# Down projection in seven block products for its first 1024 columns, with three changes of waits

## The chip, the cores and the metric

The kernel runs on the 8 cores of one Trainium2 chip. Each core computes one of 8 batch elements with the same program and exchanges nothing with the others. The metric is the device time of the slowest core in microseconds (us), as the median of several executions. The engines are named as in the profile: PE is TensorE, DVE VectorE, ACT ScalarE, POOL GpSimd, SP the queue of SyncE. POOL and SP issue the DMAs here.

## What is computed

One layer: token mixing (one projection of 2048 tokens to 9216 columns, a gated unit and block-sparse attention, an output projection), cross-attention to 256 memory tokens, and a SwiGLU block, each with RMSNorm before and after. The part that is changed most is the last matrix product.

```python
def swiglu(n, w_gate, w_up, w_down):
    return (jax.nn.silu(n @ w_gate) * (n @ w_up)) @ w_down
# n (2048 tokens, 2048), w_gate and w_up (2048, 5632), w_down (5632, 2048)
h = h + rms_norm(swiglu(rms_norm(h, ffn_pre_g), w_gate, w_up, w_down), ffn_post_g)
```

## The kernel before

The work runs in stages, in the trace in this order: input projection (to about 1003 us), attention with the memory's K and V and w_a as filler (to 1283), branch b (to 1394), output projection (to 1640), cross-attention (to about 1850), gate and up projections (to 2874), down projection (to the end). Operands are f16, sums f32 in PSUM, a bank holding 128 x 512. Every instruction goes through helpers of the Builder class (`mm` L315, `tr` L318, `act` L328, `tt` L331, `cp` L348 and L350, `dma` L357), so rows are told apart by their tiles.

**Order.** `Sched.add` keeps a program order for each engine and works out waits from Buf objects. Each engine runs its list in order, so an instruction that waits holds back all behind it. A write to a Buf that another DMA with another semaphore wrote last waits for that DMA. The stages from attention to cross-attention are ordered by `Plan.run`, a list scheduler: each task has an engine, a duration, a latency (`lat`, for a DMA the guessed time to landing), dependencies and a priority. The plan sets only the order on each engine; real waits are by semaphore. Input, gate/up and down projections are written out by hand.

**Seven products.** Input, gate and up projections already use a Strassen form (Winograd's variant). A block pair is 2 x 2 on each side; operands are A11, A12, A22, A21, the sums S1, S2, S3 (in A21's place), S4, and for the weights B11, B21, B22, T1, T2, T3 (in B12's place), T4. `quad_steps` (L947) runs the seven products of 8 matmuls of 512 columns into three banks X, Z, Y; after the first, third and fifth product into X and the fourth into Y, ACT copies the bank out (`snap`), the product goes on accumulating, and DVE adds bank and copies into the four results. It is a generator that yields after its first and second product. `mid` holds hooks that are called after the n-th product, for sums that DVE makes beside it. Results are stored when done.

**Attention's start** (`last_block`, L1210). While the last block of the input projection runs, SP issues K, Q and V of head 0 and then the four 1 MB tiles wk (weights for the memory's K and V). `f_hl` (L1354) loads K, Q and V of head 1, with lat 8. `wkl` (L1554) stands for the four wk loads in the plan; `wal` loads w_a, both first tiles at once.

**Cross-attention's start.** `f_wo` (L1932) loads the two column halves of w_co into one tile `wo` with one Buf; all output products depend on both (`lo`). `gto`, the gains that DVE needs in every eviction, is loaded after them in plan order.

**Gate and up.** 22 blocks of 256 columns, each loaded by POOL for gate and up; p is the half of the tokens (p=1 the later 1024). The loop over `quads` (L2272) begins with four quads with p=1 alone, since the plan before has done two blocks with p=0; ahead of it DVE makes the sums S1 to S4 of p=1 (`fsum`, two instructions each). Beside it POOL casts w_down to f16 in DRAM (`wd_cast`, 128 rows each time, 44 times, into WDH). The hidden values go to DRAM as HIDT, one row of 11,264 bytes per partition and token tile.

**Down.** All 2048 columns are plain: out(128 tokens, 512 columns) is 44 matmuls of 512 columns. The loop over `units` (L2323) has two parts. The first is 32 column blocks (columns 0 to 1023 of 16 token tiles), in 28 units, most with one column block, each with its own load of an `ht` tile (1408 KB) into one of three buffers; ACT copies each bank out, and it is stored to Y3. Weights lie in three sets of 44 tiles of 128x512 (W0, W1, W2), loaded in parts by POOL from WDH in runs of 1 KB. The second part goes over 16 token tiles with the column blocks 2 and 3; Y3 and the residual H2 come back (`row_pre`), and the norm and the sum are finished there.

## Time and profile before

| what | value |
|---|---|
| times of the three runs | 3480.22, 3475.23, 3486.62 us |
| median | 3480.22 us |
| the profiled execution's own time | 3503.88 us |
| its span, on core 5, the slowest | 3502.3 us |
| spans of all cores | 3456.9 to 3502.3 us |
| PE busy | 3406.8 us, 97% of the span |
| DVE, ACT, POOL busy | 1474.6, 1214.1, 237.4 us |
| matmuls of the down projection | 2816, mean 380 ns on the page |
| DMA packets' bytes | 467.89 MB |

A span is the time from the first to the last instruction of one core. Matmuls are pipelined: the duration of one (380 ns) is longer than the distance to the next (216 ns), so the cost of many is read from where a long piece starts and ends. "Idle before, releaser" is time in which the engine waited, and what ended that.

### The profile page before, as it was taken

How to read it: one execution, taken by the hardware profiler on the slowest of the kernel's cores; microseconds unless marked ns; L12 is line 12 of the kernel's file. 1: busy time of each engine (PE TensorE's matmuls, PEld its weight loads, DVE VectorE, ACT ScalarE, POOL GpSimd, SP SyncE). 2: the span in 40 equal slices, each digit the busy share in tenths (PEclk: the TensorE clock that was granted, in tenths of full speed). 3: DMA queues.
4: the chain of work that ended last, by engine and by line, in shares of the span. 5: the costliest groups of instructions: out<-in, count | busy, mean ns of one | idle time of the engine just before them, and what ended most of it. 6: DMA issues, size and time to landing. Idle time of an engine off the chain costs nothing.

```text
span 3502.3 us, 50752 instructions; the slowest of 8 cores (3456.9 to 3502.3 us)
## 1 busy us (share of the span) xinstructions
PE 3406.8 (97%) x17866; PEld 1646.4 (47%) x17866; DVE 1474.6 (42%) x2704; ACT 1214.1 (35%) x2179; POOL 237.4 (7%) x318
## 2 busy tenths in 40 slices
PE   6999999999989999999999999999999999999998
PEld 3544444444456654545744444444444444444443
DVE  4754246533237767444875343434433420001222
ACT  4643322344357740444862223232232220000111
POOL 1100000000000000000111000000000000000000
PEclk9999889999999999999999999999999999999999
DMA  7446666767663544544779767787677858577775
GB/s 177 104 67 84 94 95 109 122 111 139 107 164 90 122 135 126 164 143 163 217 199 108 86 84 94 93 93 93 76 95 90 97 156 270 151 218 210 212 223 164
DMA packets 341576, 467.89 MB, mean 134 GB/s; under 512 B 29904, under 2 KB 289232, under 8 KB 319184
## 3 DMA queue, kind: packets, MB, share of 16 engines
q0 software_dynamic: 192240, 157.30, 35.7%
q1 hardware_dynamic: 149088, 307.35, 29.7%
q8 instruction: 148, 2.42, 0.3%
q14 instruction: 100, 0.82, 0.1%
HBM read 486.62 MB, written 154.14 MB: 183 GB/s over the span
## 4 chain that ended last, share of the span: by engine, by line
PE 90%; DMA 5%; DVE 2%; issue 1%; ACT 1%; POOL 0%; SPq 0%; DVEq 0%; ACTq 0%; POOLq 0%
PE ps L315 89%; PE ps L318 1%; DMA xs<-x 1%; DMA wv<-w_in 1%; DMA H<-yr 1%; DMA ht<-HIDT 1%; DMA k<-KD 1%; DMA VD<-stg 0%; DMA gto<-gains 0%; DVE f L331 0%; DVE n1op L331 0%; ACT stg L348 0%; DVE at L341 0%; ACT no L328 0%; ACT nbh L328 0%
## 5 line engine op out<-in xcount | busy, mean ns | idle before, releaser
L315 PE MATMUL ps<-wd,ht 128*128 128x512 f16 x2816 | 611.1, 380 | 4.2 <-DMA ht<-HIDT 4.2
L315 PEld LDWEIGHTS ps<-wd,ht 128*128 128x128 f16 x2816 | 276.0, 98 | 339.1 <-issue 8.9
L348 ACT COPY fpf<-ps 128x512 f32<-128x512 f32 x336 | 197.0, 587 | 558.8 <-PE ps L315 558.8
L348 ACT COPY pf<-ps 128x512 f32<-128x512 f32 x256 | 150.3, 587 | 285.1 <-PE ps L315 285.1
L331 DVE TENSOR_TENSOR fpf<-ps,fpf 128x512 f32<-128x512 f32 x168 | 115.9, 690 | 315.5 <-PE ps L315 315.5
L315 PE MATMUL ps<-n1op,ws0r 128*128 128x512 f16 x1024 | 241.5, 390 | 2.5 <-DVE n1op L331 1.7
L315 PE MATMUL ps<-n1op,ws1r 128*128 128x512 f16 x1024 | 240.3, 389 | 0.0
L315 PE MATMUL ps<-RBH,ma 128*128 128x512 f16 x1024 | 226.2, 379 | 0.0
L328 ACT ACTIVATE pT<-ps 128x512 bf16<-128x512 f32 (+1 forms) x320 | 169.3, 543 | 73.8 <-PE ps L315 70.1
L315 PE MATMUL ps<-n1op,ws0t 128*128 128x512 f16 x768 | 183.0, 390 | 2.8 <-DVE n1op L331 1.8
L315 PE MATMUL ps<-n1op,ws1t 128*128 128x512 f16 x768 | 181.1, 387 | 0.9 <-ACT pf L348 0.6
L331 DVE TENSOR_TENSOR fpf<-fpf,fpf 128x512 f32<-128x512 f32 x84 | 58.2, 692 | 269.0 <-ACT fpf L348 269.0
L315 PE MATMUL ps<-f,fw1r 128*128 128x512 f16 x736 | 168.0, 379 | 2.2 <-DVE sm L2008 2.2
L315 PE MATMUL ps<-f,fw0r 128*128 128x512 f16 x736 | 168.1, 379 | 1.5 <-ACT fpf L348 1.5
L328 ACT ACTIVATE junk<-ps 128x512 bf16<-128x512 f32 x128 | 76.4, 597 | 264.8 <-PE ps L315 261.2
L315 PEld LDWEIGHTS ps<-n1op,ws0r 128*128 128x128 f16 x1024 | 101.6, 100 | 129.8 <-issue 33.5
L315 PEld LDWEIGHTS ps<-n1op,ws1r 128*128 128x128 f16 x1024 | 102.0, 100 | 125.8 <-issue 23.7
L331 DVE TENSOR_TENSOR yrow<-yrow,gtf 128x1024 f32<-128x1024 f32 x16 | 19.5, 1219 | 322.3 <-ACT dj L328 322.3
L315 PE MATMUL ps<-f,fw2r 128*128 128x512 f16 x672 | 151.9, 379 | 0.9 <-ACT fpf L348 0.9
L315 PEld LDWEIGHTS ps<-RBH,ma 128*128 128x128 f16 x1024 | 99.0, 98 | 113.6
L315 PE MATMUL ps<-f,fw3r 128*128 128x512 f16 x672 | 151.9, 379 | 0.0
L315 PE MATMUL ps<-at,was 128*128 128x512 f16 x512 | 150.4, 379 | 0.0
(224 smaller groups left out, 4634.3 us busy)
## 6 DMA issues: line engine op xcount, KB each, us to landing
ht<-HIDT SPq DMA_DIRECT2D x44, 1408.0 KB, 10.7
H<-yr SPq DMA_DIRECT2D x32, 1024.0 KB, 10.7
HIDT<-ffo SPq DMA_DIRECT2D x88, 256.0 KB, 5.7
WDH<-w_fd POOLq DMA_DIRECT2D x44, 512.0 KB, 20.9
ws0r<-w_in POOLq DMA_DIRECT2D x16, 1024.0 KB, 14.7
ws1r<-w_in POOLq DMA_DIRECT2D x16, 1024.0 KB, 14.5
GS<-stgh SPq DMA_DIRECT2D x64, 256.0 KB, 6.5
xr<-x SPq DMA_DIRECT2D x16, 1024.0 KB, 8.6
```

Source lines behind the costliest of these rows:

```text
L315: self.S.add("pe", lambda e: e.matmul(out, lhsT, rhs, start=start, stop=stop, **kw), reads, writes)
L318: self.S.add("pe", lambda e: e.transpose(out, in_, ident), reads, writes)
L328: self.S.add("act", lambda e: e.activation(out, in_, func, **kw), reads, writes)
L331: self.S.add(eng, lambda e: e.tensor_tensor(out, in0, in1, op), reads, writes)
L348: self.S.add("act", lambda e: e.copy(out, in_), reads, writes)
```

## The change

WDH shrinks to columns 1024 to 2047. Columns 0 to 1023 of w_down go to WD7, laid out by half of the rows (kh) and 256 columns, so that one of its blocks is 11,264 contiguous bytes per partition; each cast of 128 rows becomes two DMAs. The first part of the down stage becomes 16 calls of `down_quad`. One takes two token tiles (rows 1 and 2 of A) and 512 columns: its operands are quarters, 128 x 2816 elements (22 tiles of 128 of the hidden dimension). Each product is 22 matmuls of 256 columns. A quad loads four quarters of 704 KB, two quads ahead, and DVE makes the next quad's four sums. The weights' seven operands are three sums (`wt`) and four loaded blocks (`w7`); the first set is loaded and summed during the last gate/up quads, the second loaded in quads 1 to 4 and summed in quad 7. Columns 1024 to 2047 are computed as before, with weights W2 (loaded in quads 9 to 12) and W3 (in quad 15), three ht buffers, and an extra load order there.

The three changes of waits. Attention: two of the four wk loads come after head 1's K, Q and V, whose lat is 15; the first w_a load reads the Buf of the last wk tile. Cross-attention: the two halves of `wo` have their own Bufs, and each product depends on its half. Gate/up: before the first quad only S1 and S2 are made, quads 0 and 1 run their first two products each in turn, then S3 and S4 are made, and then the rest of both.

The core of the diff:

```diff
-    WDH = B.scratch("WDH", [HID, D], F16)
+    WDH = B.scratch("WDH", [HID, 1024], F16)
+    WD7 = B.scratch("WD7", [2, 4, 128, HC // 2 * 256], F16)
...
-        for i in range(4):
-            B.dma("sp", wk.t[i][:], WKH[i], wk.d[i], bWKH, [wk.b[i]])
+        for i in range(2):
+            load_wk(i)
+    def load_wk(i):
+        B.dma("sp", wk.t[i][:], WKH[i], wk.d[i], bWKH, [wk.b[i]])
...
-        hld.append(T("sp", 1.5, f_hl, [hld[-1]], hstart[h - 1], [(QK, ("qk", h))], lat=8.0))
+        hld.append(T("sp", 1.5, f_hl, [hld[-1]], hstart[h - 1], [(QK, ("qk", h))], lat=15.0 if h == 1 else 8.0))
...
-    wkl = [T("sp", 0.0, lambda: None, (), 0, lat=6.0 + 3.0 * i) for i in range(4)]
+    wkl = [T("sp", 0.0, lambda: None, (), 0, lat=1.0 + 4.0 * i) for i in range(2)]
+    wkl += [T("sp", 0.5, lambda i=i: load_wk(i), (), 0.1 * i, lat=6.0 + 4.5 * i) for i in (2, 3)]
...
-            cast_load(was.t[i][:].rearrange("p (k n) -> p k n", k=8), w_a, 0, GW, jp * 256, 256, was.d[i], [was.b[i]])
+            B.dma("pool", was.t[i][:].rearrange("p (k n) -> p k n", k=8),
+                  w_a[:, jp * 256:(jp + 1) * 256].rearrange("(k p) n -> p k n", p=128), was.d[i], [wk.b[3]] if jp == 0 else [],
+                  [was.b[i]])
...
-        wal.append(T("pool", 1.2, wa_load(jp), wal[-1:], FILL + jp, [(WAP, ("wa", jp))], lat=10.0))
+        wal.append(T("pool", 1.2, wa_load(jp), wal[-1:] or wkl[3:], FILL + jp, [(WAP, ("wa", jp))], lat=10.0))
...
+        return lambda: B.dma("sp", WO3[:, ch],
+                             WOH[:, ch * 1024:(ch + 1) * 1024].rearrange("(k p) n -> p k n", p=128), dwo[ch], bWOH, [wo_t.bufs[ch]])
+    lo = [T("sp", 0.5, f_wo(ch), [own], -7 + ch, lat=6.0 + 2.5 * ch) for ch in range(2)]
...
+                        B.mm(p[:], ap[:, hh * 128:(hh + 1) * 128], WO3[:, cb // 2, hh, cb % 2 * 512:(cb % 2 + 1) * 512], hh == 0, hh == 3,
+                             bufs + [wo_t.bufs[cb // 2]], [pb])
+                o_ = T("pe", 0.87, f_o, [oc, o_ if cb else None, lo[cb // 2]], tt, [(BY, bk)] + ([(YR, yk), (SM, sk2)] if cb == 0 else []),
...
+        kh, kk = r // KD2, r % KD2
+        B.dma("pool", WD7[kh, :, :, kk * 256:(kk + 1) * 256].rearrange("c p n -> p c n"),
+              w_fd[r * 128:(r + 1) * 128, 0:1024].rearrange("p (c n) -> p c n", c=4), dw7[r % 4], [], [bWD7[r]])
+        B.dma("pool", WDH[r * 128:(r + 1) * 128, :], w_fd[r * 128:(r + 1) * 128, 1024:2048], dwd[r % 4], [], [bWDH[r]])
...
+    W2 = WCol("wd2", [(0, 11), (122880, 11), (134144, 11), (145408, 11)])
+    W3 = WCol("wd3", [(163840, 11), (18432, 11), (156672, 5), (11264, 5), (120832, 1), (52224, 11)])
+    hts = [tile("ht%d" % i, o_h, HC * 128, F16, claim=False) for i, o_h in enumerate((98304, 29696, 40960))]
...
+    def hop(m, w):
+        if w in (S1, S2, S4):
+            return hs[(S1, S2, S4).index(w)]
+        return rq[m % 2][(A11, A12, A21, A22).index(w)]
+    def load_q(m, w, claim=False):
+        t_ = hop(m, w)
+        if claim:
+            t_.claim()
+        tt, kh = 2 * (m % 8) + (w in (A21, A22)), int(w in (A12, A22))
+        B.dma("sp", t_[:], HIDT[tt, :, kh * HH:(kh + 1) * HH], t_.d,
+              [bHID[b][tt // 4] for b in range(kh * NBF // 2, (kh + 1) * NBF // 2)], [t_.b])
+    def load_w7(g, i, after=()):
+        kh, c = i // 2, 2 * g + i % 2
+        B.dma("pool", w7[g][i][:], WD7[kh, c], w7[g][i].d, bWD7[kh * KD2:(kh + 1) * KD2] + list(after), [w7[g][i].b])
+    def hsum(m, which):
+        o, a_, b_, op = ysum[which]
+        O, A_, B_ = hop(m, o), hop(m, a_), hop(m, b_)
+        B.tt(O[:], A_[:], B_[:], op, [A_.b, B_.b], [O.b])
+    def wsum(g, which):
+        b11, b12, b21, b22 = w7[g]
+        O, A_, B_ = {"T1": (wt[0], b12, b11), "T3": (b12, b22, b12), "T2": (wt[1], b22, wt[0]), "T4": (wt[2], b21, wt[1])}[which]
+        for c in range(2):
+            cs_ = slice(c * WH // 2, (c + 1) * WH // 2)
+            B.tt(O[:, cs_], A_[:, cs_], B_[:, cs_], ALU.subtract, [A_.b, B_.b], [O.b])
     def pre_down():
-        W0.claim()
-        W0.load(0)
-        hts[0].claim()
-        load_unit(0)
+        for t_ in w7[0]:
+            t_.claim()
+        for i in (1, 0, 3, 2):
+            load_w7(0, i)
+        load_q(0, A11, True)
+        load_q(0, A12, True)
...
-    for w_ in ("S1", "S2", "S3", "S4"):
+    for w_ in ("S1", "S2"):
...
+            mid = {4: lambda: fprep(2), 6: lambda: fprep(3)}
         elif qi == 1:
-            mid = {2: lambda: fsum(0, "S1"), 4: lambda: fsum(0, "S2"), 6: lambda: fsum(0, "S3")}
+            mid = {4: lambda: fsum(0, "S1"), 5: lambda: fsum(0, "S2"), 6: lambda: fsum(0, "S3")}
         elif qi == 2:
             mid = {1: lambda: fsum(0, "S4")}
         if p == 1 and 0 < b < NBF - 2:
             mid[4] = lambda b=b, w=w: fprep((2 * b + 2 + w) % 4)
         if b == NBF - 2 and p == 0:
             mid[4] = lambda w=w: fprep((2 * NBF - 2 + w) % 4)
+        if (b, w, p) == (NBF - 1, 0, 1):
+            mid = {2: lambda: wsum(0, "T1"), 5: lambda: wsum(0, "T3")}
+        if (b, w, p) == (NBF - 1, 1, 1):
+            mid = {2: lambda: (hs[0].claim(), hs[1].claim(), hsum(0, "S1")), 3: lambda: hsum(0, "S2"),
+                   5: lambda: (wt[1].claim(), wsum(0, "T2")), 6: lambda: hsum(0, "S3")}
...
+        if qi < 2:
+            pair.append(quad_steps(ops, p, add, direct, mid))
+            if qi == 0:
+                continue
+            for g_ in pair:
+                next(g_)
+                next(g_)
+            for w_ in ("S3", "S4"):
+                fsum(1, w_)
+            for g_ in pair:
+                for _ in g_:
+                    pass
+        else:
+            quad(ops, p, add, direct, mid)
...
+            wt[0].claim()
+            load_q(0, A21, True)
+            load_q(0, A22, True)
+    for w_ in (A11, A21, A22, A12):
+        load_q(1, w_, True)
+    wt[2].claim()
+    hs[2].claim()
+    hsum(0, "S4")
+    wsum(0, "T4")
+    for t_ in w7[1]:
+        t_.claim()
...
+    def load_unit(u):
+        h_ = hts[u % 3]
+        if u < 3:
+            h_.claim()
+        B.dma("sp", h_[:], HIDT[u], h_.d, [bHID[b][u // 4] for b in range(NBF)], [h_.b])
+    ns = [0]
+    def down_quad(m):
+        g = m // 8
         mark = Buf("unit")
-        if ui == NA_:
-            yrow = rot("yrow", [32768, 40960], D, F32)
-            hr = rot("hr", [49152, 57344], D, F32)
-            row_pre(0)
-        if ui >= NA_ and t + 1 < NT:
+        X, Z, Y = ps_next(), ps_next(), ps_next()
+        W = w7[g] + wt
+        o_ = [yst.tiles[yst.i % 4], yst.tiles[(yst.i + 1) % 4]]
+        yst.i += 2
+        hooks = {}
+        def hook(n, f):
+            hooks.setdefault(n, []).append(f)
+        def prod(bank, a, wi, start):
+            a_, w_ = hop(m, a), W[wi]
+            for k in range(KD2):
+                B.mm(bank[0][:, 0:256], a_[:, k * 128:(k + 1) * 128], w_[:, k * 256:(k + 1) * 256], start and k == 0, k == KD2 - 1,
+                     [a_.b, w_.b], [bank[1], mark] if wi == 0 and k == 0 else [bank[1]], skip_group_check=True)
+            n = prod_n[0] = prod_n[0] + 1
+            for f in hooks.get(n, ()):
+                f()
+        prod_n = [0]
+        def snap(bank):
+            t_, b_ = snp[ns[0] % 6]
+            ns[0] += 1
+            B.cp(t_[:], bank[0][:, 0:256], [bank[1]], [b_], eng="act")
+            return t_, b_
+        def add(i, l, a, b):
+            t_ = o_[i]
+            B.tt(t_.t[:, l * 256:(l + 1) * 256], a[0][:, 0:256], b[0][:, 0:256], ALU.add, [a[1], b[1]], [t_.bufs[l]])
+        def store(i):
+            t_, tt = o_[i], 2 * (m % 8) + i
+            B.dma("sp", Y3[tt * 128:(tt + 1) * 128, g * 512:(g + 1) * 512], t_.t[:], t_.d, t_.bufs, [bY3[tt][g]])
+        if m == 7:
+            hook(4, lambda: (wsum(1, "T1"), wsum(1, "T2"), hsum(8, "S1"), hsum(8, "S2")))
+            hook(5, lambda: (wsum(1, "T3"), hsum(8, "S3")))
+            hook(6, lambda: hsum(8, "S4"))
+            hook(7, lambda: wsum(1, "T4"))
+        elif m < 15:
+            hook(4, lambda: [hsum(m + 1, w_) for w_ in ("S1", "S2", "S3")])
+            hook(6, lambda: hsum(m + 1, "S4"))
+        if m < 14:
+            hook(5, lambda: [load_q(m + 2, w_) for w_ in (A11, A21, A12)])
+            hook(7, lambda: load_q(m + 2, A22))
+        if m in (1, 2, 3, 4):
+            hook(1, lambda: load_w7(1, m - 1, [mark]))
+        if m in (9, 10, 11, 12):
+            hook(1, lambda: W2.load_part(2, m - 9, [mark]))
+        if m == 15:
+            hook(1, lambda: [W3.load_part(3, i) for i in (2, 3, 4)])
+            hook(1, lambda: load_unit(0))
+            hook(2, lambda: (yrow.tiles[0].claim(), hr.tiles[0].claim(), row_pre(0)))
+            hook(3, lambda: (load_unit(1), W3.load_part(3, 0)))
+            hook(4, lambda: W3.load_part(3, 1))
+            hook(5, lambda: (gtf.claim(), B.dma("sp", gtf[:], gains[2:3, :].partition_broadcast(128), gtf.d, [], [gtf.b])))
+            hook(7, lambda: W3.load_part(3, 5))
+            hook(7, lambda: load_unit(2))
+        prod(X, A11, 0, True)
+        s1 = snap(X)
+        prod(Z, A12, 2, True)
+        add(0, 0, Z, s1)
+        prod(X, S2, 5, False)
+        s2 = snap(X)
+        prod(Y, S1, 4, True)
+        s5 = snap(Y)
+        prod(X, A21, 1, False)
+        s3 = snap(X)
+        add(1, 1, s5, s3)
+        prod(Y, S4, 3, False)
+        add(0, 1, Y, s2)
+        store(0)
+        prod(X, A22, 6, False)
+        B.cp(o_[1].t[:, 0:256], X[0][:, 0:256], [X[1]], [o_[1].bufs[0]], eng="act")
+        store(1)
+    for m in range(16):
...
+        down_quad(m)
+    dj.claim()
+    yrow.tiles[1].claim()
+    hr.tiles[1].claim()
+    Wc = {2: W2, 3: W3}
+    for t in range(NT):
+        if t and t + 2 < NT:
+            load_unit(t + 2)
+        if t + 1 < NT:
```

## Rows read from the trace of the kernel before

**Rows 1.** Cores: span and mean granted clock of two of them.
```profile
core 3: 3467.9 us, clock 0.995
core 5: 3502.3 us, clock 0.983
```

**Rows 2.** The page's chain that ended last, shares by engine and by line.
```profile
PE 90%; DMA 5%; DVE 2%; issue 1%; ACT 1%; POOL 0%; SPq 0%; DVEq 0%; ACTq 0%; POOLq 0%
```

**Rows 3.** Waits of PE, core 5: releaser: us in total, times, longest.
```profile
PE ps L315 <- DVE kmt L335: 8.6, 1, 8.6
...
PE ps L315 <- DMA ht<-HIDT: 4.2, 2, 3.6
```

**Rows 4.** Chain in time, core 5, down stage: start us, us, what.
```profile
3162.98 12.46 PE ps L315 x44
...
3185.51 304.07 PE ps L315 x1408
```

**Rows 5.** Instructions with tile ht, core 5: duration ns min/median/max, first and last start.
```profile
L315 PEld LDWEIGHTS ps<-wd,ht x2816: 95/98/147, 2874.1 to 3489.0; 128*128 128x128 f16 x188
L315 PE MATMUL ps<-wd,ht x2816: 376/379/631, 2874.3 to 3489.2; 128*128 128x512 f16 x188
```

**Rows 6.** Chain in time, core 3, from 2800 us.
```profile
2800.00 331.10 PE ps L315 x1534
```

**Rows 7.** PE's timeline, core 5, cross-attention: start us, us, instruction.
```profile
1659.26 0.39 PE L315 MATMUL ps<-kvs,cpt 128*128 128x129 bf16 x4
1659.49 1.91 PE L315 MATMUL ps<-ma,wq 128*128 128x256 f16 x16
1661.24 1.03 PE L315 MATMUL ps<-wo,cot 128*128 128x512 f16 x4
```

**Rows 8.** Timelines of PE and DVE, start of the gate/up quads.
```profile
1851.77 3.62 PE L315 MATMUL ps<-f,fw0r 128*128 128x512 f16 x16
1858.27 5.12 PE L315 MATMUL ps<-f,fw0t 128*128 128x512 f16 x16 [2.88 <-DVE f L331]
1864.85 3.61 PE L315 MATMUL ps<-f,fw0r 128*128 128x512 f16 x16 [1.47 <-ACT fpf L348]
...
1907.38 3.62 PE L315 MATMUL ps<-f,fw0r 128*128 128x512 f16 x16
...
1852.72 10.14 DVE L331 TENSOR_TENSOR f<-f,f 128x2048 f16<-128x2048 f16 x8
```

**Rows 9.** The page's costliest groups: busy us, mean ns, idle before.
```profile
L331 DVE TENSOR_TENSOR fpf<-ps,fpf 128x512 f32<-128x512 f32 x168 | 115.9, 690 | 315.5 <-PE ps L315 315.5
```

**Rows 10.** Stages, core 5: busy of PE, PEld, DVE, ACT, POOL; clock, DMA share, GB/s.
```profile
2893.00:2912.00 19.00, 19.00 (x90) 8.61 (x88) 0.00 (x0) 1.17 (x2) 2.14 (x2) 1.00 1.01 327
...
2931.00:2950.00 19.00, 19.00 (x90) 8.62 (x88) 0.00 (x0) 1.17 (x2) 0.95 (x1) 1.00 0.87 249
```

**Rows 11.** DMA issues: queue, count, KB each, median us to landing.
```profile
wd<-WDH POOLq DMA_DIRECT2D x4, 1408.0 KB, 17.6
...
WKH<-w_ckv POOLq DMA_DIRECT2D x16, 256.0 KB, 17.4
```

**Rows 12.** Chain and PE's timeline, core 5, first microseconds of attention.
```profile
1004.54 19.70 DMA k<-KD
...
1027.87 0.35 PE L315 MATMUL ps<-kmt,q 128*128 128x8 bf16 x8 [8.65 <-DVE kmt L335]
...
1028.90 1.06 PE L315 MATMUL ps<-memT,wk 128*128 128x256 f16 x4
```

**Rows 13.** SP's and PE's timelines and the chain, start of cross-attention.
```profile
1632.45 7.82 SPq L357 DMA_DIRECT2D wo<-WOH  x2
...
1646.53 1.87 PE L315 MATMUL ps<-wo,cot 128*128 128x512 f16 x4 [2.37 <-DMA wo<-WOH]
...
1656.23 1.89 PE L315 MATMUL ps<-wo,cot 128*128 128x512 f16 x8 [0.60 <-DVE yr L331]
...
1642.23 13.00 DMA gto<-gains
```

More of the change, by code:

```diff
@@ L498, in _program @@
     bWDH = [Buf("WDH") for _ in range(HC)]
+    bWD7 = [Buf("WD7") for _ in range(HC)]
     bWKH = [Buf("WKH") for _ in range(KC)]
@@ L503, in _program @@
     bHID = [[Buf("HID") for _ in range(NTG)] for _ in range(HC // 2)]
-    bY3 = [Buf("Y3") for _ in range(NT)]
+    bY3 = [[Buf("Y3") for _ in range(2)] for _ in range(NT)]
     M = Mem(nc)
@@ L1724, in _program @@
     junk_r = tile("junk", 202752, 512, BF16)
-    wo_t = tile("wo", 163840, 8192, F16, claim=False)
-    WO3 = wo_t[:].rearrange("p (k n) -> p k n", k=4)
+    wo_t = tile("wo", 163840, 8192, F16, claim=False, parts=2)
+    WO3 = wo_t[:].rearrange("p (c k n) -> p c k n", c=2, k=4)
     gto = tile("gto", 180224, D, F32, claim=False)
@@ L2232, in load_part @@
                   bWDH[k:k + n] + list(after), [b_])
-        def load(self, cb):
-            for i in range(len(self.parts)):
-                self.load_part(cb, i)
-    W0 = WCol("wd0", [(122880 + i * 10240, 10) for i in range(4)] + [(0, 4)])
-    W1 = WCol("wd1", [(65536 + i * 11264, 11) for i in range(4)])
-    W2 = WCol("wd2", [(163840 + i * 10240, 10) for i in range(4)] + [(110592, 4)])
-    hts = [tile("ht%d" % i, o_h, HC * 128, F16, claim=False) for i, o_h in enumerate((4096, 16384, 49152))]
@@ new lines, in _program @@
+    wt = [tile("wt%d" % i, o_, WH, F16, claim=False) for i, o_ in enumerate((18432, 163840, 52224))]
+    W2 = WCol("wd2", [(0, 11), (122880, 11), (134144, 11), (145408, 11)])
[5 more added lines that the diff above has]
+        return rq[m % 2][(A11, A12, A21, A22).index(w)]
@@ L2318, in row_pre @@
         ht_, hb, hd = hr.next()
[L2319 removed]
+        B.dma("sp", y[:, 0:1024], Y3[t * 128:(t + 1) * 128, :], yd, bY3[t], [yb])
         B.dma("sp", ht_[:], H2[t * 128:(t + 1) * 128, :], hd, [bH2[t]], [hb])
         rows[t] = (y, yb, ht_, hb, hd)
[L2323 to L2340 removed]
+    def load_unit(u):
[3 more added lines that the diff above has]
+        B.dma("sp", h_[:], HIDT[u], h_.d, [bHID[b][u // 4] for b in range(NBF)], [h_.b])
@@ new lines, in _program @@
+    for m in range(16):
[8 more added lines that the diff above has]
+        if t + 1 < NT:
+            row_pre(t + 1)
+        h_ = hts[t % 3]
+        y, yb, ht_, hb, hd = rows[t]
+        s, sbf, _ = sm.next()
+        B.act(dj[:], y[:, 0:1024], AF.Square, [yb], [dj.b, sbf], accum=s[:, 2:3])
+        B.tt(y[:, 0:1024], y[:, 0:1024], gtf[:, 0:1024], ALU.mult, [yb, gtf.b], [yb])
+        for ci, cb in enumerate((2, 3)):
@@ L2372, in _consts @@
+        np_ = 4 if t == NT - 1 else 1
+        for q in range(np_):
+            cs_ = slice(q * D // np_, (q + 1) * D // np_)
+            hq, hqd = hb, hd
+            if np_ > 1:
+                hq, hqd = Buf("hrq"), B.dsem("fin%d" % q)
+                hq.last_w = hb.last_w
+            B.stt(ht_[:, cs_], y[:, cs_], s[:, 6:7], ht_[:, cs_], ALU.mult, ALU.add, [yb, sbf, hq], [hq])
+            B.dma("sp", out[t * 128:(t + 1) * 128, cs_], ht_[:, cs_], hqd, [hq], [Buf("o")])
 def _consts():
```

104 lines of the change are left out of this document (25 added, 79 removed).

## The prediction, made before the change was run

> **What bounds the kernel now.** I read the spans of the cores first [rows 1]: the profiled execution was measured on core 5, 34 us longer than core 3, at a mean granted clock of 0.983 against 0.995. So what the change gives has to be worked out as a difference, and by stage. Next the page's chain that ended last: 90% of it is TensorE, 89% matmuls of one line [rows 2]. So the time is the sum of what TensorE streams and the gaps in it. The list of TensorE's waits and the chain show those that the change aims at: one DVE wait of 8.6 us at 1027.87 and two waits for ht tiles [rows 3].
>
> The down projection is the last stage. Its matmuls begin at 2874.3 and its second half, 1408 matmuls, runs unbroken in 304.07 us [rows 4, 5]: 0.2160 us per 512-wide matmul. The first half has the same 1408 matmuls and takes 3185.51 - 2874.3 = 311.2 us: 7.1 us are lost, 4.2 waiting for two tiles and 3.0 because 44 matmuls after the first wait took 12.46 us and not 9.5 [rows 3, 4]. On core 3 the chain shows 1534 matmuls in one piece of 331.10 us there, 0.2158 us each [rows 6], so this loss is not on every core.
>
> **Part 1, the products.** Removed: 1408 matmuls of 512 columns, 304.1 us. Added: 16 quads x 7 products x 22 matmuls of 256 columns, 2464 in all. Nothing in the trace runs 256-wide for long; the nearest row has 16 in a row, from 1659.49 to 1661.24 [rows 7]: 1.75 us, 0.1094 us each. 2464 x 0.1094 = 269.5 us. So -34.6 us. From below I bound the price at half of 0.2160 (266.1 us, 3.4 less), from above by the same 16-row plus a tenth, since long 256-wide stretches aren't shown (+27). I take the row itself.
>
> TensorE's weight load has 98 ns on the row of the same matmuls [rows 5], shorter than 109, and the 129-wide matmuls, four in 0.23 us [rows 7], show that loads need not space matmuls at 98. The Trainium skill, "TensorE: Matmul & The Clock Gate", section "Back-to-back issue gap", speaks against the change: it gives sustained spacings of 131 ns at 512 columns and 81 ns at 128, so by a straight line 98 at 256, and the change would cost 2464 x 98 - 1408 x 131 ns = 57 us more. The trace disagrees at the wide end, with 216 ns over 1408 matmuls. It is the third rival.
>
> **Part 2, the adds beside it.** Per quad DVE gets four sums of 128x2816 f16. A 128x2048 f16 sum takes 10.14 / 8 = 1.27 us [rows 8]; by length 1.7. With three evictions' adds of at most 0.69 [rows 9] that is some 9 us in a quad of 154 x 0.1094 = 16.85 us: covered. ACT has five copies of half a bank in those 16.85 us. Snapshots have a whole other product (2.4 us) to happen in. Twice DVE also makes the weight sums, eight halves of 1.7 us = 13.6. The first set is made in the last gate/up quads; its last sum is queued behind S3 and S4, and I count it done 11 us into the stage, needed at 14.4 (after six products). The second set, in quad 7, gives DVE about 22 us of work in a 16.85 us quad. By my queue its last sum is done at 30.8 us from that quad's start, and product 7 of quad 8 asks at 16.85 + 6 x 2.41 = 31.3. The store of quad 7 waits for a DVE add behind those sums, and SP has the load of the next A22 behind that store. So 0.5 us for both, 0 to 3.
>
> **Part 3, the transfers.** A quad loads four quarters of 0.72 MB and stores 0.52 MB: 3.4 MB in 16.85 us, 202 GB/s; in eight quads 1.44 MB of weights come on top: 4.85 MB, 288 GB/s. The trace shows 327 GB/s with the engines full, just after this stage began [rows 10], with no TensorE wait there. So steady quads fit. Quad 15 is different. From 2.4 us into it to the use of the last weight part (33.5 us) the code issues W3's 5.8 MB, three ht tiles (4.3), two rows of Y3 and H2 (3.1), gtf (1.0) and stores (0.5): 14.7 MB in 31 us, 473 GB/s, more than 327. If both queues share evenly, the POOL queue's 5.8 MB at 160 GB/s end at 38.4 us, 4 us late after the part before was 1 us late; W1's parts, 1408 KB each, issued 9.5 us apart in the full stretch, landed in 17.6 us [rows 11], which fits that rate. SP's tiles are wanted later. A wait costs clock as well (3.0 us after the ht wait above). I take 4 us here, 0 to 10.
>
> The two ht waits with their clock go (-7.1), since a quarter's load now starts 14 us or more before its sum is wanted and its first product needs it 9 us after that. Together the stage gives -34.6 - 7.1 + 4.5 = **-37.2 us** on core 5.
>
> **Part 4, the casts.** WDH's cast becomes two DMAs per 128 rows, one writing 512-byte pieces, so 44 more POOL issues of about 1 us each, beside weight loads that are issued two blocks ahead of use. A cast of this shape, WKH, lands in 17.4 us [rows 11]; the last is issued two quads (24 us) before the first load that needs it. Cost 0; if the cover is short, 2.
>
> **Part 5, the start of the gate/up quads.** In the trace TensorE runs two products from 1851.77, waits 2.88 us for DVE, which is making eight sums (1852.72, 10.14 us), runs 16 matmuls in 5.12 us, waits 1.47, and reaches the fifth quad at 1907.38 [rows 8]. Four quads are 224 x 0.216 = 48.4 us; they took 55.6: 7.2 lost. Now four products (6.9 us) come first and only S1 and S2 before them, done at 6.0 us. S3 follows two adds and is done at 10.1, wanted at 10.4; S4 at 12.7, wanted at 12.1. I leave 1.2 us of loss: **-6 us** (-3 to -7). What is late next is S4, by 0.6.
>
> **Part 6, the start of attention.** Head 1's K is issued at 1004.54 behind four 1 MB loads and lands 19.70 us later; DVE, in order, waits for it with oT and acc work queued behind, and TensorE waits 8.65 us, then runs at the lower clock level, 1.2 GHz, for some us: four 256-wide matmuls still take 1.06 us a microsecond later [rows 12], so I add an estimated 1.3 us for the clock. Now two of those loads come behind K, and the planner puts K's reductions 7 us later. K then has 2 MB less before it, 7 us at 280 GB/s, and lands near 1012, before DVE asks. Gone: 8.65 + 1.3. Against it: w_a's load now waits for the last wk tile, so filler for TensorE is thin between the second and third wk tile and until w_a lands. A stretch of 10 us in which ACT sets the pace at nine tenths costs 1 us. **-8.7 us** (-2 to -12).
>
> **Part 7, the start of cross attention.** The second wo load waits on SP for the first, 7.82 us for the pair; TensorE waits 2.37 us for it at 1646.53. But gto lands at 1655.23 and DVE's four evictions begin only then; TensorE waited 0.60 at 1656.23 for a free bank [rows 13]. Without the wo wait TensorE merely comes to that bank sooner. Only what gto gains counts: 1 MB less beside it at about 300 GB/s is 3 us, if SP still reaches it behind the H store. **-2 us** (+1 to -5).
>
> **Sum**, against the profiled execution's own 3503.9 us: -37.2 - 6 - 8.7 - 2 = -53.9, giving 3450. The median of the runs shown is 3480.2, between a core like 3 (span 3468, without the ht loss, so about -47) and core 5. I take -52 for it: **3428 us**.
>
> **The rivals.** (a) *Transfers set the down stage.* For it: quarters, weights and stores ask 288 GB/s in half of the quads, and some 30 us later the same kinds of transfer moved 249 GB/s at a share of 0.87 [rows 10]. Against it: that was what was asked then, not the limit. At 250 GB/s each such quad takes 19.4 us, 2.55 too long, 20 us in eight, and quad 15's backlog 8 more: 3456. (b) *The waits move.* The wait for K becomes thin filler, wo's becomes gto's, S4 replaces S2; parts 5 to 7 give 5 us instead of 17: 3440. For it: in-order queues with a plan whose times are guesses; against: each removed wait has a named cause that is gone. (c) *The 256-wide matmul doesn't keep its price*, the rival on the slower side: if weight load and matmul don't overlap when the next one is only 256 long, the price rises from 109 towards 98 + 107 = 205 ns. The products alone break even at 304.1 / 2464 = 123 ns, the whole change at about 130; at 145 ns the stage takes 357 us and the kernel 3516. Against it are the 16 in a row at 109. (d) *The change doesn't do what it says*: if the second DVE set stalls every product of quad 8 and the sums run behind the products in all quads, DVE bounds; at 9 us of 16.85 it has room, and I give this no more than its share in (a).
>
> **Chances.** Forecast 0.60, (b) 0.20, (a) 0.15, (c) 0.05. Unknown terms around the forecast: products -3, quads 7 and 15 -4.5 to +8, attention -3 to +7, gto -3 to +3, cores +5 to -2. The range is 3408 to 3456; it holds the forecast and (b) and a part of (a). About 0.3%, 10 us, is what a measurement of this kernel can tell from no change: faster by more 0.94, within it 0.02, slower 0.04.
>
> **What would show it.** In the profile after: 2464 matmuls of 128x256 with hq or hs tiles, unbroken pieces at 0.109 us each and a first half of 270 to 278 us; a wait for wd at the second 512-wide column of the first row tile, if quad 15 is as I count it; no kmt wait over 2 us; the fifth gate/up quad within 50 us of the first; gto landing before 1655 us by the clock of the profile before, minus what was gained ahead of it. Wrong would be a spacing above 0.115, waits for hq spread over quads 1 to 4 and 9 to 12, or a lower granted clock in the new stage.

## The result and the profile after

In the first comparison the changed kernel took 3449.8 us in the median of the runs and the kernel before 3483.4; the ratio is 0.9899, 95% interval [0.9854, 0.9943]. A second comparison, on another chip, gave 0.9961 [0.9885, 1.0038]. In single executions one pair of cores is often granted less clock for some hundred microseconds and then alone sets the time, in both kernels. So the sharper measure on that second chip is the span of all cores whose mean granted clock was 0.992 or more: 3464.9 us for the kernel before (66 spans), 3430.4 us for the changed one (28 spans). The change gives **-34.5 us** by that measure; with the bound at 0.98 it would be -27.3, at 0.995 -38.3. Forecast were -52 and 3428 us. The 3449.8 us lie inside the range of 3408 to 3456, but 22 us above the forecast and nearer to the times of the rivals (b), 3440, and (a), 3456. On the second chip the median was 3485.9 us, against 3510.6 for the kernel before: the time itself is in the range only on a chip like the first.

The cores of the profiled execution, as in [rows 1]; core 0 set the time; the spans lie within 27 us of each other, where the kernel before had 45:

```profile
core 0: 3448.6 us, clock 0.992
...
core 2: 3421.6 us, clock 0.995
```

The chain that ended last, from the page, beside [rows 2]. DMA holds the same share, and the weight parts (wd) are new in it:

```profile
PE 90%; DMA 5%; DVE 2%; issue 2%; ACT 1%; POOL 0%; DVEq 0%; SPq 0%; ACTq 0%; POOLq 0%
PE ps L315 88%; PE ps L318 2%; DMA VD<-stg 1%; DMA wv<-w_in 1%; DMA wd<-WDH 1%; DMA xs<-x 1%; DMA H<-yr 0%; DMA hq<-HIDT 0%; DMA gto<-gains 0%; DVE n1op L331 0%; DVE f L331 0%; DVE at L341 0%; ACT no L328 0%; ACT nbh L328 0%; ACT stg L348 0%
```

TensorE's waits from gate/up on, core 0 (releaser: us in total, times, longest), beside [rows 3]. The waits for ht are gone, and so is the one for kmt earlier in the span; the longest from here on are for wd:

```profile
PE ps L315 <- DMA wd<-WDH: 10.5, 3, 6.3
PE ps L315 <- ACT fpf L348: 3.1, 2, 2.8
PE ps L315 <- DMA hq<-HIDT: 0.8, 1, 0.8
```

The down stage on core 0, the chain in order of time (start us, us, what), beside [rows 4]. First the seven products, then the last 1024 columns:

```profile
2868.99 249.95 PE ps L315 x2288
```

```profile
3079.85 39.09 PE ps L315 x358
...
3119.49 28.19 DMA wd<-WDH
...
3147.81 32.32 PE ps L315 x149
```

2288 matmuls of 256 columns in 249.95 us are 0.1092 us each. The groups of that stage by shape (line, engine, operation, count | busy us, mean ns of one | idle before) show what ran beside them, a weight load of 98 ns under each and sums of 1.62 us on DVE:

```profile
L315 PE MATMUL ps<-w,hq 128*128 128x256 f16 x1056 | 120.7, 273 | 0.8 <-DMA hq<-HIDT 0.8
L315 PEld LDWEIGHTS ps<-w,hq 128*128 128x128 f16 x1055 | 103.2, 98 | 13.1 <-issue 1.0
...
L331 DVE TENSOR_TENSOR hq<-hq,hq 128x2816 f16<-128x2816 f16 x16 | 25.9, 1618 | 0.0
```

Two stretches of core 0 around the last weight part (busy time of PE, PEld, DVE, ACT, POOL; granted clock, DMA share, GB/s), beside [rows 10]: in the first the DMA engines are full while TensorE stands 9 us, in the second they are at half:

```profile
3110.00:3145.00 35.00, 26.14 (x155) 15.13 (x154) 2.77 (x4) 2.97 (x8) 3.20 (x3) 0.90 1.00 346
3145.00:3180.00 35.00, 33.39 (x156) 14.99 (x155) 9.63 (x12) 5.05 (x12) 1.11 (x2) 1.00 0.45 169
```

In the first stretch the two queues moved this (packets, MB, share of the 16 engines' time; q1 is SP's queue, q0 POOL's):

```profile
q1 hardware_dynamic: 1326, 7.92, 64.8%
q0 software_dynamic: 1052, 4.16, 34.8%
```

The start of gate/up, TensorE's timeline, beside [rows 8]. The third group of seven products waits 2.85 us before its fifth product, where the kernel before waited 0.93 us (core 0):

```profile
1854.31 3.62 PE L315 MATMUL ps<-f,fw2r 128*128 128x512 f16 x16
1857.76 3.62 PE L315 MATMUL ps<-f,fw2t 128*128 128x512 f16 x16
1864.22 3.61 PE L315 MATMUL ps<-f,fw2r 128*128 128x512 f16 x16 [2.85 <-ACT fpf L348]
```

and DVE's timeline there: the eviction's sum at 1862.20, for which that copy waited, comes behind the sums of 128x2048 for the next row of products, two instructions for each sum.

```profile
1859.73 2.55 DVE L331 TENSOR_TENSOR f<-f,f 128x2048 f16<-128x2048 f16 x2
1862.20 0.68 DVE L331 TENSOR_TENSOR fpf<-ps,fpf 128x512 f32<-128x512 f32 x1
```

The stages, in us. Before are the profiled execution's cores other than 4 and 5 (mean), after the same cores in the second comparison's profiled execution, in which, as before, just cores 4 and 5 were late; the last column is the forecast, made on core 5.

| stage | before | after | difference | forecast |
|---|---|---|---|---|
| attention, first product of head 0 to the next projection | 277.5 | 270.8 | -6.7 | -8.7 |
| cross-attention to the first gate/up group of the loop | 218.4 | 215.0 | -3.4 | -2 |
| first two gate/up groups, 14 products | 30.5 | 25.4 | -5.1 | |
| rest of gate/up | 992.2 | 994.8 | +2.6 | -6 for both |
| down, first 1024 columns | 305.9 | 269.4 | -36.5 | -41.2 |
| down, last 1024 columns | 303.9 | 315.2 | +11.3 | +4 |
| sum | | | -37.8 | -53.9 |

The spans of these cores differ by 36.5 us in those two executions.

### The profile page after: what moved, and what is told of

Its sections match the earlier page's. It is cut to its first block, busy times and chain, and to the rows that moved or that the text cites. A ratio compares the mean times of both kernels' runs of the same rounds, so it can differ in the third digit from the quotient of the medians.

```text
span 3448.6 us, 53547 instructions; the slowest of 8 cores (3421.6 to 3448.6 us)
## 1 busy us (share of the span) xinstructions
PE 3341.7 (97%) x18882; PEld 1743.2 (51%) x18922; DVE 1618.3 (47%) x2832; ACT 1224.0 (35%) x2227; POOL 267.0 (8%) x361
## 4 chain that ended last, share of the span: by engine, by line
PE 90%; DMA 5%; DVE 2%; issue 2%; ACT 1%; POOL 0%; DVEq 0%; SPq 0%; ACTq 0%; POOLq 0%
PE ps L315 88%; PE ps L318 2%; DMA VD<-stg 1%; DMA wv<-w_in 1%; DMA wd<-WDH 1%; DMA xs<-x 1%; DMA H<-yr 0%; DMA hq<-HIDT 0%; DMA gto<-gains 0%; DVE n1op L331 0%; DVE f L331 0%; DVE at L341 0%; ACT no L328 0%; ACT nbh L328 0%; ACT stg L348 0%
## 5 line engine op out<-in xcount | busy, mean ns | idle before, releaser
L315 PE MATMUL ps<-wd,ht 128*128 128x512 f16 x1408 | 306.0, 380 | 10.5 <-DMA wd<-WDH 10.5
L315 PE MATMUL ps<-n1op,ws0r 128*128 128x512 f16 x1024 | 234.1, 381 | 2.5 <-DVE n1op L331 1.6
L315 PEld LDWEIGHTS ps<-wd,ht 128*128 128x128 f16 x1408 | 137.9, 98 | 178.2 <-issue 13.8
L315 PE MATMUL ps<-wv,n1op 128*128 128x512 f16 x512 | 121.8, 390 | 11.7 <-DMA wv<-w_in 7.9
## 6 DMA issues: line engine op xcount, KB each, us to landing
ws0r<-w_in POOLq DMA_DIRECT2D x16, 1024.0 KB, 13.9
```

The source lines that it names most:

```text
L315: self.S.add("pe", lambda e: e.matmul(out, lhsT, rhs, start=start, stop=stop, **kw), reads, writes)
```

## The experiments

The first set, of four, and the third, of three, ran on chips on which most cores were granted clocks of 0.93 to 0.97, with the kernel before too; there I read waits, single stages and, in the third set, cores 4 to 7, which had 0.984 or more. The second set had full clock.

### The changes of waits alone

The kernel before with these edits of the change (wk loads in two steps, w_a behind the last of them, wo in two halves with a Buf each, the first two gate/up groups interleaved), for instance:

```diff
-        for i in range(4):
-            B.dma("sp", wk.t[i][:], WKH[i], wk.d[i], bWKH, [wk.b[i]])
+        for i in range(2):
+            load_wk(i)
```

> The kernel before with the three changes of waits alone; the down projection keeps its 512-wide matmuls. Theory (the stages add up, each change of waits is worth what its stage showed in the changed kernel): attention 270 to 272 us where the kernel before has 276 to 280 (-7), cross-attention and the row statistics 213 to 218 us for 218 (-3.6), the start of gate/up -3 (30.5 us falls to 25.4, of which 2.3 or more come back at the third group of four products), the down projection unchanged at 304 to 311 us for its first half. Sum -13 to -14 us, 0.996 of the time before. Rival A (waits move): what the three stages gain comes back as waits in the gate/up or down stage, the time is within 3 us of the time before. Rival B (the input stage pays): the first attention matmul starts some 9 us later than in the quiet cores of the kernel before (966 to 975 us), as it did in the changed kernel, because of the moved loads; then the time is -4 us.

Measured in the first set: 3693.4 us against 3687.6, a difference lost in the spread of both (3651 to 4089 and 3665 to 3993). So it was taken to another chip:

> The kernel of waits only (before, with the three changes of waits and no seven-product down projection) again, on another chip, since on the first all cores from 2 to 7 ran at a granted clock of 0.93 to 0.97 in both kernels and the ratio was 1.0016. Theory (stages add up at full clock): -10 to -14 us, 0.996 to 0.997 of the kernel before. Rival (what the stages gain is given back later, as the ratio on the first chip suggests): 0.999 to 1.002, and in the trace a later stage is longer by 8 us or more than in the kernel before.

Measured: 0.9954 [0.9895, 1.0014]; by the spans of cores at 0.992 or more, 3450.9 us (44 spans) against 3464.9, **-14.0 us**. Attention took 268 to 271 us, cross-attention 211 to 214, the first two gate/up groups 25.4, the rest of gate/up 994.1 to 995.8, and the down projection 608 to 611 in all. The interval of the ratio includes no change, so the -14.0 rests on the spans and the stages. The stages show every gain that the changed kernel had, and nothing was given back behind gate/up, so rival A falls. The first attention matmul started at 969 to 978 us, 2 us later in the mean than in the quiet cores of the kernel before and not 9, so rival B falls.

### The down projection alone

The changed kernel with those edits undone.

> The changed kernel with the three changes of waits undone: the down projection's first 1024 columns by seven products alone. Theory: sixteen groups of matmuls take 269 to 270 us where the kernel before took 305 to 311 for the same columns (-37), the last 1024 columns take 314 to 316 us for 304 (+11, waits for the last weight parts); attention 276 to 280, cross-attention 218, the start of gate/up 30.5 as before. Sum -26 us, 0.9925. With the kernel of waits only this adds up to the changed kernel's measured -34 to -40. Rival A (the new scratch in device memory slows the input stage): the first attention matmul starts at 970 to 990 us, 9 us later in the mean than in the quiet cores of the kernel before, and the sum is -17 us. Rival B (the narrow matmuls cost more when the earlier stages are as before, by the granted clock): the sixteen groups take over 272 us.

Measured in the first set: 3671.1 us against 3687.6, -17. The place of the loss in the last columns is the same as in the changed kernel: TensorE waits 4.6 to 8.7 us by core for wd. What I had not expected is the granted clock. Core 0 by stage (columns as above): gate/up in two halves, the seven products, the last columns.

```profile
1888.00:2390.00 502.00, 502.00 (x2315) 226.83 (x2314) 196.69 (x293) 148.62 (x249) 55.22 (x70) 0.99 0.66 92
2390.00:2890.00 500.00, 499.74 (x2279) 224.60 (x2278) 196.85 (x286) 144.80 (x243) 47.35 (x61) 0.98 0.61 97
2890.00:3177.00 287.00, 287.00 (x2466) 249.85 (x2464) 135.45 (x126) 29.40 (x79) 10.86 (x13) 0.93 0.73 244
3177.00:3491.00 314.00, 306.38 (x1411) 138.15 (x1409) 78.22 (x92) 39.98 (x95) 9.28 (x16) 0.98 0.55 207
```

The seven-product stage alone ran at 0.93, without a wait, and took 287 us for 269. In the waits-only kernel of the same set, core 2, the same columns with 512-wide matmuls had 0.99, like the gate/up stage in front of them:

```profile
2386.00:2891.00 505.00, 505.00 (x2316) 227.79 (x2315) 188.78 (x284) 148.10 (x248) 35.81 (x43) 0.99 0.58 97
2891.00:3202.00 311.00, 310.16 (x1425) 139.88 (x1424) 1.08 (x2) 18.72 (x32) 13.42 (x14) 0.99 0.64 214
3202.00:3513.00 311.00, 311.00 (x1393) 138.59 (x1391) 78.20 (x92) 39.70 (x94) 8.23 (x15) 0.96 0.56 201
```

Cores 4 to 7 of the down-only kernel had 0.92 to 0.93 in gate/up, 0.88 in the seven products and 0.91 to 0.92 behind. Rival B's number, over 272 us, came out on every core (287 to 302 us). But the kernel with the weight parts in SP's queue, which has the changes of waits, took 284 to 300 us there on the same chip, so it belongs to this chip's clock and not to the earlier stages. Rival A has no support: the first attention matmul started at 1005 to 1029 us here and at 1014 to 1044 in the waits-only kernel of the set, which lacks the new scratch. The kernel was run once more:

> The seven-product down projection alone again (the changed kernel with its three changes of waits undone), wanted at full clock: on the first chip the cores ran at granted clocks of 0.93 to 0.97 and the ratio was 0.9955. Theory: sixteen groups 269 to 271 us for the 305 to 311 of the kernel before, the last 1024 columns 314 to 316 for 304, so -26 us or 0.9925; with the waits-only kernel's 0.9954 that makes the product 0.988 of the changed kernel. Rival (the two parts give the same time twice, as the cores wait for each other nowhere and the sum should hold only if no wait is shared): the sum of both misses the changed kernel's gain by over 8 us.

This chip was no full-clock one either. 3604.0 us against 3615.3. On cores 4 and 5 the seven products took 274 us, on cores 6 and 7, where the granted clock was 0.95 in that stage and 0.99 to 1.00 in gate/up, 281.8; the last columns 314 to 316. The waits the other part removes are there again (kmt 4.0 to 7.9 us on cores 4 to 7). The full-clock price of this part alone was not measured. As the difference of two measured gains it is 34.5 - 14.0 = 20.5 us, and by stages of the changed kernel 36.5 - 11.3 = 25.2. Neither can test the rival of a shared gain, since both take the sum for granted: whether the two parts add up within 8 us stays open. For it speaks only that they lie in different stages.

### The row loads behind the sixteen groups

```diff
-            hook(2, lambda: (yrow.tiles[0].claim(), hr.tiles[0].claim(), row_pre(0)))
-            hook(3, lambda: (load_unit(1), W3.load_part(3, 0)))
+            hook(3, lambda: W3.load_part(3, 0))
...
     for m in range(16):
         down_quad(m)
+    load_unit(1)
+    ...
```

> The changed kernel, but the row loads that SP issues beside the last group's weight parts (the second and third token tile's transposed rows of 1408 KB, the first residual row, the gains) are issued only behind the sixteen groups. The bytes needed by the end of the kernel are the same. Theory A (the two queues compete, and the queue with the long rows takes the larger part, so that the last 1408 KB weight parts, which landed in 27 us, come too late): the parts land in under 20 us, TensorE's three waits for them (2.5, 6.3 and 1.6 us) go, and the last 1024 columns take 304 to 308 us instead of 314 to 316; -8 to -10 us against the changed kernel. The second token tile's rows then come in time (19 us of matmuls for the first tile) or cost up to 3 us. Theory B (the weight parts are late by their own number of bytes and the late release of their buffers, whatever runs beside them): the last columns still take 312 us or more, same time as the changed kernel. Theory C (the wait moves): the weight waits go and waits of 5 us or more for the second and third token tile's rows appear in their place.

Measured in the first set: 3639.6 us against 3687.6 for the kernel before and 3671.1 for the down projection alone. The waits for wd were 1.0 to 4.2 us by core where the down-only kernel of that set had 4.6 to 8.7, and no wait for ht or hq appeared. Theory A holds in direction, C falls. The changed kernel was not in this set, so what the edit gives in time was not measured. What is left is one wait, and the chain of core 0 shows why: the last part is issued when the last product is done, and the moved loads are now issued beside it.

```profile
3189.92 38.89 PE ps L315 x353
...
3229.35 20.18 DMA wd<-WDH
```

### The weight parts in SP's queue

```diff
-            hook(1, lambda: [W3.load_part(3, i) for i in (2, 3, 4)])
+            hook(1, lambda: [W3.load_part(3, i, q="sp") for i in (2, 3, 4)])
```

and so for the other parts.

> The changed kernel, but the last weight parts are issued by SP, in one line with the row loads, instead of by POOL: the same bytes from the same points on. Theory A (division between the queues decides): in one queue the weight parts that are issued first are served first; parts 1408 KB each land in 10 to 20 us instead of 27, the weight waits of 10.5 us shrink below 4 us, the row loads land later and cost nothing before the second token tile; the last columns take 306 to 310 us instead of 314 to 316. Theory B (bytes in front of a due time decide: 44 us from the last group's start are needed for all of them whatever the order): the last columns take 313 us or more. Theory C (SP stands still at the buffer of a weight part and holds back the row loads behind it): waits of over 5 us on the token tiles' rows.

Measured in the first set: 3647.1 us, waits for wd 2.7 to 8.9 us by core. That did not tell the theories apart, so:

> The last weight parts issued by SP in one line with the row loads, again at full clock; on the first chip TensorE's waits for them came to 3.5 to 8.9 us by core where the kernel with POOL's own queue had 4.6 to 8.7. Theory A (division between the two queues is what made the last part late, since SP took 69% of the bytes): waits under 4 us, the last columns in 306 to 309 us. Theory B (what counts is how many bytes are asked for in front of the last part; one line or two gives nearly the same): waits of 6 to 11 us, the last columns in 311 to 316 us, so that only taking loads out from in front of the part, as in the version with the row loads behind it (303.7 us), helps.

Measured: 3577.7 us against 3615.3; on cores 4 to 7 waits for wd of 5.2 to 8.9 us and 315 to 319 us for the last columns. The chain of core 5:

```profile
3114.93 9.54 SPq L357
...
3125.00 8.58 SPq L357
...
3134.41 16.38 DMA wd<-WDH
```

In one queue the last part lands 16.4 us after its issue and not 28, but SP spends 9.5 and 8.6 us on two issues in front of it, so it is issued later: 3150.8 is where it lands. Theory A falls in its effect. B's ranges, 6 to 11 us and 311 to 316 us, are met on some cores and missed narrowly on others. But the run is no clean test of the division, for the points of issue moved: POOL had issued the first three parts, 1.4 MB, 10 to 14 us ahead of the last group, and SP, in order, issues them 1.5 to 2.5 us into it; the last part is issued 24 to 28 us into it instead of 17.5. What it shows is that one queue did not help. SP did stand still, as C has it, but no token tile's rows were waited for.

### The last part first, and the sums spread

```diff
+    w5 = [W3.parts[5][3]]
+    row_pre(0, w5)
+    B.dma("sp", gtf[:], gains[2:3, :].partition_broadcast(128), gtf.d, w5, [gtf.b])
+    load_unit(2)
...
-            mid = {4: lambda: fsum(0, "S1"), 5: lambda: fsum(0, "S2"), 6: lambda: fsum(0, "S3")}
+            mid = {4: lambda: fsum(0, "S1"), 6: lambda: fsum(0, "S2")}
-            mid = {1: lambda: fsum(0, "S4")}
+            mid = {6: lambda: fsum(0, "S3")}
+        elif qi == 3:
+            mid = {6: lambda: fsum(0, "S4")}
```

The loads in the first block stood in the last group before, beside the weight parts.

> The changed kernel with two edits: the first residual row, the gains and the third token tile's transposed rows are fetched only when the last weight part has landed; and the vector engine's sums for the next row of products (the first product sums of the gate) are spread over the second to fourth groups instead of three in the second. Theory A (too much is asked of the DMA engines in front of the last weight part; 3.9 MB less in front of it, worth 12 us at the 310 to 400 GB/s of those stretches): the last part lands within 10 to 16 us of its issue instead of 28, TensorE's waits for it fall from 10.5 us to under 2, and the last columns take 305 to 308 us for 316; the wait of 2.9 us at the third group of the gate goes, too. Sum -10 to -13 us against the changed kernel, 0.996 to 0.997 of it. Theory B (the part is late because of its late release alone): the wait stays over 4 us there, sum -4. Theory C (the wait moves): the sums spread over later groups stop the fifth group, or the vector engine, which multiplies by the late gains first, holds the products' buffers so that TensorE waits for them; the sum is 0 to -3.

Measured: a ratio of 0.9825 [0.9774, 0.9875] against the kernel before, 3428.6 us in the median; 3413.2 us by the cores at 0.992 or more (48 spans), **-17.2 against the changed kernel and -51.7 against the one before**. The last columns took 303.6 to 303.7 us on all cores, -11.5, and gate/up behind its first two groups 991.5, -3.3; the third group's wait there is 0.3 us. The chain of core 0, in the stretch that had the 28 us for wd, is one piece, and the waits (releaser: us in total, times, longest) have no wd:

```profile
3049.91 120.28 PE ps L315 x753
```

```profile
PE ps L315 <- DMA hq<-HIDT: 0.4, 1, 0.4
PE ps L315 <- ACT fpf L348: 0.3, 1, 0.3
```

The three 1408 KB parts land in 11.3 us (median, core 0; 25.2 in the changed kernel of the same set):

```profile
wd<-WDH POOLq DMA_DIRECT2D x3, 1408.0 KB, 11.3
```

Theory A holds on both edits. B falls: the last part was issued 17.5 us into the last group, as before, and landed in time on every core. C falls, too: DVE, which multiplies by the gains first, stood 24.5 us for them and nothing on TensorE noticed. Which of the two edits gave what can be read from the stages, since they lie in different ones. The remaining 2 us beyond the stages' 14.8 are within what cross-attention varies by.

### The changed kernel again

> The changed kernel once more, beside the others of this set on one chip. It is the mark against which the next kernel's stages are read, and it asks whether the later start of the first attention matmul (970 to 990 us by core against 966 to 975 us in the quiet cores of the kernel before) belongs to the change. Theory (it belongs to the single profiled executions: waits of TensorE for operands that were stored and fetched again early on, which vary between executions): here the start lies anywhere from 966 to 990 us, other kernels of the set likewise, and the measured difference to the kernel before is larger than the first 34 us, up to 44. Rival (a cost of the change): the start is again 9 us later in the mean than that of kernels without the new scratch, and the difference stays at 34.

This is the second comparison above. Its first attention matmul started at 968 to 975 us on six cores and at 1007 on two whose granted clock was 0.96 until then; in the first profiled execution of the same kernel it was 970 to 990, with waits of 1.1 to 13.1 us by core for stg tiles, which DVE fills and which are stored to VD (here 0.5 to 7.5). On core 0 DVE itself had stood 44 us there until such stores had landed (here 22). The later start belongs to the execution and not to the change; there the rival falls. My theory failed in its other half: it had the difference grow beyond 34 us, up to 44, and it stayed at 34.5.

### w_a's load early again

```diff
-            B.dma("pool", was.t[i][:]..., was.d[i], [wk.b[3]] if jp == 0 else [], [was.b[i]])
+            cast_load(was.t[i][:]..., w_a, 0, GW, jp * 256, 256, was.d[i], [was.b[i]])
```

> The changed kernel with one of its edits undone: the first half of the next projection's weights is loaded by POOL as early as before, beside the key weights, instead of behind the last of them. Theory (the wait for the key weights went because only two of the four are asked for at the stage's start, and POOL's load was no rival of theirs): attention stays at 269 to 274 us, no change in time. Rival (POOL's load had been what held the key weights back): TensorE waits 2 to 8 us at the first product of the keys again on some cores and attention takes 273 us or more in the mean, +3 to +7 us.

Measured: 3603.4 us against 3615.3, attention 273.1 to 281.2 us on cores 4 to 7, where the kernel with the weight parts in SP's queue, of the same set, had 269.3 to 269.5. The waits-only kernel of the second set had 268 to 271 and the changed kernel 269 to 274. kmt's wait did not come back; TensorE waits 2.2 to 8.4 us by core for wk in its place, on core 6 of this kernel:

```profile
PE ps L315 <- DMA wk<-WKH: 7.1, 1, 7.1
```

```profile
989.77 22.31 DMA wk<-WKH
```

I had expected no change, and the rival holds: with w_a's load beside them, asking for wk in two steps only moved the wait from kmt to wk, and the stage takes what it took before (275.9 to 280.5 us). The gain hangs on w_a's load coming later. Whether that alone would give it, with all four wk loads first, was not run.

## Why the prediction was right, and where not

**The products (Part 1)** were right: 0.1092 us against 0.1094 taken from a row of 16, and 269.5 us on the mean of all eight cores as worked out. At full clock rival (c) has no support. Neither have the Trainium skill's sustained spacings ("TensorE: Matmul & The Clock Gate", "Back-to-back issue gap"), with 216 ns measured at 512 columns and 109 at 256. Rival (c) was on the mark in another way, below.

**The waits for ht (Part 3)** were the wrong size. -7.1 was core 5's own loss. The six cores of the table took 304.8 to 306.7 us for that half, 305.9 in the mean where the second half takes 303.9, so this term was worth 2.0 there. Likewise kmt's wait, 8.6 on core 5, was 4.4 to 8.3 us on those six cores, 6.2 in the mean. The first was the price of a late core, the second in part, and I set both against a median that other cores make.

**The last group's transfers (Part 3)** were the larger error, +4 forecast and +11.3 measured. The place was right, the second 512 columns of the first row tile, and so was the size of the backlog (14.7 MB forecast; 13.9 MB landed from 3100 to 3150 us on core 0). The step that failed is "if both queues share evenly", with all of POOL's 5.8 MB starting 2.4 us into the group. POOL issued the first 1.4 MB 10 to 14 us ahead of the group. Of the rest, 4.3 MB were issued from 8 us into it and took until its 46th, 115 GB/s and not 160; from 3110 to 3145 us POOL's queue moved 34% of the bytes. The last part was used 44 to 46 us by core after the group's start, not 38.4, and 8.3 us of the 11.3 were waits for it and the part before (six cores, mean). With 3.9 MB taken out from in front of it and the same point of issue it landed in time on every core, so that was what made it late. Moving the parts to the other queue did not help, but there they were also issued later. The prediction had the number that was enough: 14.7 MB at the 346 GB/s measured here take 42.5 us, an estimate that gives 45 us from the group's start without any division.

**The start of gate/up (Part 5)** gave 2.5 us of the 6. The interleaving did what was worked out (-5.1, with S4 late by 0.57 on core 0). But "what is late next is S4, by 0.6" stopped too early: the third group's wait of 2.85 us came from the sums for the next row of products, which the change puts behind the later products of the second group and the first of the third. Spread over three groups, they cost 0.3 us; rest of gate/up 991.5 us. So the sign "fifth quad within 50 us of the first" was missed: it came after 52.4 us on core 0.

**Attention (Part 6)** -6.7 for -8.7 (its own terms, 8.65 + 1.3 - 1, add up to 8.95). The edit named as a cost ("w_a's load now waits for the last wk tile, so filler for TensorE is thin") was one that the gain hangs on. **Cross-attention (Part 7)** -3.4 for -2: the waits for wo (0.2 to 4.8 us by core) went, and those for yr behind gto grew from 1.3 to 4.3 to some 4 to 7, as the part said. **Casts (Part 4)** and **DVE's sums (Part 2)**: output projection 240.3 us as before, sums 1.62 us for 1.7, no wait for a sum of the down stage.

**The rivals.** (a) was right about the backlog of the last group and wrong about the steady groups, which ran unbroken at 256 GB/s. (b) happened in part: in gate/up by another operand than S4, and in cross-attention at yr. (c) is wrong at full clock and partly right below it: at a granted clock of 0.88, 302 us for 2464 matmuls are 0.1226 us each, about the 123 ns at which the products break even with full-clock 512-wide ones. There, though, those take longer too: the waits-only kernel took 323 to 325 us for the same columns on these cores, and the down projection alone still gave -11 and -17 us against the kernel before.

**The sum.** Of the 16 us between -53.9 and -37.8, the last columns explain 7.3, the first 1024 columns (the ht waits) 4.7, gate/up 3.5 and attention 2.0, less 1.4 for cross-attention. Apart from that 1.4 no errors cancelled: the products, the one large term, were right, and nearly every smaller gain was taken too large.

## What to carry to other kernels

When a stage is made shorter or denser, add up the bytes that are asked for in front of the last transfer that the next stage needs, and move behind its landing all that is wanted later; here that gave 11.5 us, and moving the last transfers to the other queue gave nothing. A helper engine's work in order has to be followed past the first wait that a change removes, to the work for the next row. And price a wait on the cores that will set the time after, not on the one that happened to be late.

## What the hardware showed

- On the two chips that granted less than full clock, the stage of 256-wide matmuls, with a weight load for each and DVE half busy, was granted less than gate/up in front of it on nearly every core, mostly by 3 to 5 points (0.93 behind 0.98; 0.88 behind 0.92; 0.95 behind 0.99; on four cores 1 point or none). The same columns with 512-wide matmuls had no such drop (0.99 behind 0.99; 0.93 to 0.94 behind 0.93). On the full-clock chips the new stage had 1.00 on every core. Whether the denser weight loads, the sums or the transfers do it was not tried.
- With both queues busy, from 3110 to 3145 us on core 0, SP's moved 7.9 MB and POOL's 4.2 MB, at 346 GB/s in sum.
- A 1408 KB weight part took 27 us with SP's queue moving 7.9 MB in 35 us beside it and 10 to 13 us (by core) with 3.9 MB fewer asked for in front of it. In one queue the last one took 16 us, where SP then spent up to 9.5 us on an issue.
- In the stretch of the late weight part the granted clock was 0.90, in that behind it 1.00: the last columns lost 11.3 us with 8.3 us of waits in them (six cores, mean).
